# Eps inside the first part's statistics, logits scaled ahead of the shift, and the eighth gathered group on VectorE

## The reference, cut to what matters

```python
def layer_norm(x, g, b):
    mu = xf.mean(-1, keepdims=True)
    var = jnp.square(xf - mu).mean(-1, keepdims=True)
    return ((xf - mu) * lax.rsqrt(var + LN_EPS) * g + b).astype(x.dtype)

def route(xf, router_w, router_b):
    s = jax.nn.sigmoid((xf @ router_w).astype(jnp.float32))
    sb = (s + router_b).reshape(T, N_GROUPS, EXP_PER_GROUP)
    g_sel = jnp.argmax(lax.top_k(sb, 2)[0].sum(-1), axis=-1)      # best group of 8 experts
    ...                                                           # then the best two experts in it
def reference(...):
    for l in range(DEPTH):                                        # DEPTH = 2
        mix = hybrid_mixer(x, ...)
        x = layer_norm(ALPHA * x + mix, ln1_g[l], ln1_b[l])
        ffn = moe_ffn(x, router_w, router_b, moe_w1[l], moe_w3[l], moe_w2[l])   # 64 experts, 1024 -> 256 -> 1024
        x = layer_norm(ALPHA * x + ffn, ln2_g[l], ln2_b[l])
    return x
```

## Time and profile before

| | |
|---|---|
| three runs | 1145.03, 1145.22, 1147.53 us; median 1145.22 |
| profiled execution | 1146.11 us, of which 1143.2 us are the span from the first instruction to the last |
| busy, share of the span | PE 91%, PEld 50%, DVE 35%, ACT 24%, POOL 2% |
| DMA | 440.82 MB, mean 386 GB/s |
| the chain that ended last | PE 81%, DMA 10%, DVE 6%, issue 2% |
| mean granted TensorE clock | 0.993 |

### The profile page before, as it was taken

One profiled execution on the slowest core, in us unless ns is written; L12 is line 12 of the kernel. 1 busy time (PEld: TensorE's weight loads), 2 busy tenths in 40 slices (PEclk: granted clock), 3 DMA queues, 4 the chain that ended last, 5 costly groups with the idle time before them and its releaser, 6 DMA issues.

```text
span 1143.2 us, 32566 instructions
## 1 busy us (share of the span) xinstructions
PE 1045.1 (91%) x14230; PEld 573.9 (50%) x14230; DVE 405.7 (35%) x1207; ACT 270.9 (24%) x714; POOL 18.7 (2%) x36
## 2 busy tenths in 40 slices
PE   9999998899899899888899999988998998999887
PEld 6665754444445444444456657444454444444443
DVE  4875442222223222212268656322222222222223
ACT  1245331111121211111132544221212211111111
POOL 0010000000000000000000100000000000000000
PEclk9999999999999999989999999999999999999999
DMA  9968799999999999999996687999999999999997
GB/s 306 331 253 294 271 378 424 428 428 429 428 429 428 427 431 428 429 428 430 389 316 230 256 296 295 414 425 428 428 428 429 428 428 428 429 427 428 430 428 265
DMA packets 72047, 440.82 MB, mean 386 GB/s; under 512 B 16192, under 2 KB 39872, under 8 KB 45376
## 3 DMA queue, kind: packets, MB, share of 16 engines
q1 hardware_dynamic: 71712, 439.52, 94.1%
q0 software_dynamic: 144, 0.58, 0.1%
q10 hardware_dynamic: 144, 0.07, 0.0%
HBM read 439.10 MB, written 1.05 MB: 385 GB/s over the span
## 4 chain that ended last, share of the span: by engine, by line
PE 81%; DMA 10%; DVE 6%; issue 2%; SPq 1%; another core or an unknown queue 1%; ACT 0%; POOL 0%; DVEq 0%
PE bank L1179 16%; PE bank L1191 9%; PE bank L1070 9%; PE bank L1100 8%; PE bank L703 8%; PE bank L1090 8%; DMA w_even<-in_moe_w 4%; DMA w_odd<-in_moe_w 4%; PE bank L829 4%; PE bank L1142 3%; DVE moe L1696 2%; DVE moe L1754 1%; PE bank L974 1%; PE bank L1185 1%; DMA w_even<-in_w_in 1%
## 5 line engine op out<-in xcount | busy, mean ns | idle before, releaser
L1827 ACT ACTIVATE moe<-bank 128x512 f32<-128x512 f32 (+2 forms) x164 | 84.0, 523 | 546.8 <-PE bank L1090 227.3
L1696 DVE COPY moe<-bank 128x512 f32<-128x512 f32 (+1 forms) x66 | 44.6, 675 | 315.5 <-PE bank L1090 209.9
L1191 PE MATMUL bank<-moe 128*128 128x512 f32 (+1 forms) x264 | 119.5, 593 | 25.4 <-DVE moe L1754 22.5
L1070 PE MATMUL bank<-moe,x 128*64 128x64 f32 x3840 | 122.8, 224 | 3.7 <-issue 3.7
L1070 PEld LDWEIGHTS bank<-moe,x 128*64 128x64 f32 x3840 | 118.4, 139 | 6.9 <-issue 6.9
L1179 PE MATMUL bank<-w_even,moe 64*32 64x512 f32 x896 | 100.7, 598 | 10.4 <-DVE moe L1713 9.3
L1179 PE MATMUL bank<-w_odd,moe 64*32 64x512 f32 x896 | 99.6, 590 | 10.7 <-DVE moe L1713 8.7
L1987 ACT ACTIVATE moe<-bank,small 128x64 f32<-128x64 f32 x240 | 74.2, 414 | 110.5 <-PE bank L1070 110.5
L1191 PEld LDWEIGHTS bank<-moe 128*128 128x128 f32 x264 | 47.3, 189 | 99.7 <-DVE moe L1754 47.9
L1754 DVE COPY moe<-bank 128x512 f32<-128x512 f32 x28 | 19.3, 691 | 196.2 <-PE bank L1179 196.2
L703 PE MATMUL bank<-w_even,w_odd 128*128 128x384 f32 x240 | 81.3, 489 | 0.0
(11 more groups left out here) (202 smaller groups left out, 978.4 us busy)
## 6 DMA issues: line engine op xcount, KB each, us to landing
w_odd<-in_moe_w SPq DMA_DIRECT2D x86, 2048.0 KB, 29.3
w_even<-in_moe_w SPq DMA_DIRECT2D x82, 2048.0 KB, 30.4
w_even<-in_moe_w SPq DMA_DIRECT2D x28, 1024.0 KB, 8.8
w_even<-in_w_in SPq DMA_DIRECT2D x24, 768.0 KB, 10.8
w_odd<-in_moe_w SPq DMA_DIRECT2D x16, 1024.0 KB, 8.2
w_odd<-in_w_out SPq DMA_DIRECT2D x2, 2048.0 KB, 16.1
w_odd<-in_w_out SPq DMA_DIRECT2D x4, 1024.0 KB, 9.0
w_odd<-in_moe_w SPq DMA_DIRECT2D x8, 512.0 KB, 11.1
```

The lines of the kernel that those rows point to most:

```text
L1070: last = mm(bank[2 + h][64 * z:64 * z + 64, 64 * c:64 * c + 64], xc_pair[:, t, h, c, :], chosen_pair[:, t, z], start=t == 0, stop=t == 1)
L1191: return mm(Y[t][h][:, lo - 512 * h:hi - 512 * h], scatter[:, t * P:(t + 1) * P], y_rows[:, lo:hi], start=False, stop=True, skip_group_che ...
L1696: return nc.vector.tensor_copy(partial[:, k, cols], source[:, cols])
L1827: return fn(dst, src, ACT.Copy)
```

## The change

1. **Eps.** A new `add_eps(t, eps)` adds eps x 1024 to the sum of squares in the first part's statistics, right after that part's `bn_stats`. `moments` no longer adds eps; `bn_aggr` itself signals GpSimd, which reads the variance from `mean_var`. This holds for the two normalisations of both layers.
2. **Scores.** The logits are scaled first, and the shift is computed behind that with a signal of its own, `n_shift_ok`, for which ScalarE waits before it normalises the tile.
3. **Gather.** Group 7 goes to bank 6, which is otherwise unused at that time. VectorE scales it after its four others; ScalarE is left with 2, 3 and 6. The first product of the batch waits for groups 4 and 5 by `first_late_sb`, for 6 by `xg_act`, for 7 by `xg_dve`.
4. **Dummies.** Three instead of five ahead of the wait for `picked`.

```diff
+        first_part = [of[:, lo * P:(lo + 1) * P] for of, lo in ((bank[2], 0), (bank[2], 1), (bank[3], 0), (bank[3], 1),
+                                                                (bank[1], 2), (bank[1], 3), (bank[0], 2), (bank[6], 0))]
...
-                powers(1, 4, 1)
-                powers(2, 5, 1)
+                powers(1, rstd[:, 4:5], mean_var[:, 0, 1:2])
+                powers(2, rstd[:, 5:6], mean_var[:, 1, 1:2])
...
-                keep_warm(5, bank[7])
+                keep_warm(3, bank[7])
...
                         elif c == 4:
-                            pe.wait_ge(xg_dve.sem, b0 + 1)
+                            after(pe, l, first_late_sb, 1)
                         elif c == 6:
                             pe.wait_ge(xg_act.sem, b0 + 1)
+                        elif c == 7:
+                            pe.wait_ge(xg_dve.sem, b0 + 1)
...
-                def moments(t, o, eps, parts=2):
-                    link(nc.vector.bn_aggr(mean_var[:, t, :], stats[:, t, 0:parts, :].rearrange("p i s -> p (i s)")))
-                    ts(ms[:, o:o + 1], mean_var[:, t, 1:2], eps, None, ALU.add).then_inc(pow_in.sem, 1)
+                def add_eps(t, eps):
+                    link(ts(stats[:, t, 0, 2:3], stats[:, t, 0, 2:3], eps * DM, None, ALU.add))
+                def moments(t, n, parts=2):
+                    nc.vector.bn_aggr(mean_var[:, t, :], stats[:, t, 0:parts, :].rearrange("p i s -> p (i s)")
+                                      ).then_inc(pow_in.sem, 1)
+                    after(v, l, pow_in, n)
 
                 def scores(t):
                     after(v, l, pow_out, 2 + t)
-                    link(ts(shift[:, t:t + 1], mean_var[:, t, 0:1], rstd[:, 4 + t:5 + t], -1.0, ALU.mult, ALU.mult))
                     after(v, l, z_psum, t + 1)
                     after(v, l, logit_bias_ok, 1)
-                    signal(stt(out=ez[:, t, :], in0=bank[0][:, t * NE:(t + 1) * NE], scalar=rstd[:, 4 + t:5 + t],
-                               in1=logit_bias, op0=ALU.mult, op1=ALU.add), z_lin, t + 1)
+                    stt(out=ez[:, t, :], in0=bank[0][:, t * NE:(t + 1) * NE], scalar=rstd[:, 4 + t:5 + t],
+                        in1=logit_bias, op0=ALU.mult, op1=ALU.add).then_inc(z_lin.sem, 1)
+                    ts(shift[:, t:t + 1], mean_var[:, t, 0:1], rstd[:, 4 + t:5 + t], -1.0, ALU.mult, ALU.mult
+                       ).then_inc(n_shift_ok.sem, 1)
...
                 scale_first(4)
-                scale_first(5).then_inc(xg_dve.sem, 1)
+                scale_first(5).then_inc(first_late_sb.sem, 1)
+                v.wait_ge(gathered[1].sem, b0 + 1)
+                scale_first(7).then_inc(xg_dve.sem, 1)
...
                     fn(sg[:, t, :], ez[:, t, :], ACT.Sigmoid).then_inc(z_squashed.sem, 1)
+                    after(act, l, n_shift_ok, t + 1)
...
                 act.wait_ge(gathered[1].sem, b0 + 1)
-                scale_first(6)
-                scale_first(7).then_inc(xg_act.sem, 1)
+                scale_first(6).then_inc(xg_act.sem, 1)
```

More of the change, by code:

```diff
@@ L572, in _, with powers @@
             for l in range(DEPTH):
-                def powers(i, lo, n):
+                def powers(i, to, of):
                     after(pool, l, pow_in, i + 1)
-                    nc.gpsimd.tensor_tensor(rstd[:, lo:lo + n], ms[:, lo:lo + n], const("minus_half", 0, n),
-                                            ALU.pow).then_inc(pow_out.sem, 1)
-                powers(0, 0, 4)
+                    nc.gpsimd.tensor_tensor(to, of, const("minus_half", 0, of.shape[1]), ALU.pow).then_inc(pow_out.sem, 1)
+                powers(0, rstd[:, 0:4], ms[:, 0:4])
                 after(pool, l, router_in, 32)
@@ L609, in _ @@
                 total(pt(fold_mem[0], router[:, 0:4, :], router[:, 4:8, :], ALU.add), fold_mem[0][:, 0, :]).then_inc(sums_ok.sem, 1)
-                powers(1, 4, 1)
-                powers(2, 5, 1)
+                powers(1, rstd[:, 4:5], mean_var[:, 0, 1:2])
+                powers(2, rstd[:, 5:6], mean_var[:, 1, 1:2])
                 assert steps[0] == POOL_STEPS, steps
-                powers(3, 6, 1)
-                powers(4, 7, 1)
+                powers(3, rstd[:, 6:7], mean_var[:, 0, 1:2])
+                powers(4, rstd[:, 7:8], mean_var[:, 1, 1:2])
         @block.tensor
@@ L1038, in gather_first @@
                             after(pe, l, *((routed, 1) if t else (z_lin, 2)))
-                        last = mm(first_bank[c // 2][:, c % 2 * P:(c % 2 + 1) * P], xc[:, t, c, :], chosen[:, t, :],
-                                  start=t == 0 and c in (0, 2), stop=t == 1, skip_group_check=True)
+                        last = mm(first_part[c], xc[:, t, c, :], chosen[:, t, :],
+                                  start=t == 0 and c in (0, 2, DC - 1), stop=t == 1, skip_group_check=True)
                         if t == 1 and c % 2:
@@ L1651, in copy_gathered @@
                     last.then_inc(xg_dve.sem, 1)
-                for h in range(2):
-                    link(add_mix(0, h))
-                moments(0, 4, LN_EPS)
+                link(add_mix(0, 0))
+                add_eps(0, LN_EPS)
+                link(add_mix(0, 1))
+                moments(0, 2)
                 link(nc.vector.memset(find_one, BIG))
@@ L1663, in _ @@
                 link(add_mix(1, 0))
+                add_eps(1, LN_EPS)
                 signal(place(0), chosen_first, 1)
@@ L1666, in _ @@
                 link(add_quarter(3))
-                moments(1, 5, LN_EPS, 3)
+                moments(1, 3, 3)
                 weigh_scores(0)
@@ L1790, in _ @@
                     after(v, l, y_part, t + 1)
-                    part_sums(t, 0)
+                    link(part_sums(t, 0))
+                    add_eps(t, LN_EPS / ALPHA ** 2)
                 for t in range(NT):
```

11 lines of the change are left out of this document (6 added, 5 removed).

## The result

The changed kernel takes **1227.12 us** (median of five runs, 1223.00 to 1231.37) beside 1147.2 us for the kernel before on the same chip (five runs, 1145.03 to 1149.33): 1.0691 times the time, interval 1.0669 to 1.0713. The prediction said 1144.6 us with a range up to 1146.9. It forecast a gain of 0.6 us, and the change costs 80.

A forecast was written before the change was run, and what follows sets the result against it. Each layer was taken as a stretch bound by TensorE, then one bound by weight transfers. The terms summed to 2 x (0.06 + 0.14) + 0.19 = 0.59 us, from 1145.22 to 1144.6 us, range 1143.4 to 1146.9.

The forecast's parts named there:

- The step that failed: Ahead of the pick in the router: two dummies less hold back nothing and buy nothing, taken as 0.
- My slower rival: Router: TensorE's clock falls in the gap the dummies leave; up to 6.8 - 0.6 us lost, 1150 to 1151; chance 0.06.
- An instruction saved inside the batches is worth nothing: Batches of experts: DMA engines are full there, share 1.01, so saving an instruction gains nothing.
- What counts is when the stream starts: Router's end: issuing the weight load sooner than 148.16 moves the whole stream forward, until the last batch.
- `add_eps`: Both normalisations, both layers: eight small VectorE operations of 0.15 us, covered by waits; cost taken as nothing.
- Eps: Router, tile 1: without the eps addition in the chain GpSimd starts 0.18 us sooner.
- Scores: Router, tile 1: logits' scaling waits for the products, 0.12 us after their end; gain 0.06 us, bounds 0 and 0.43.
- Shift and gates: Router, behind the logits: the two VectorE instructions overlap and stay inside 0.40 us; taken as nothing, 0.10 us at worst.
- The eighth group: Gather: VectorE scales group 7, ready sooner than before; gain 0.14 us, bounds 0.05 and 0.25.
- The end of layer 0: Second normalisation, tile 0: GpSimd starts sooner, and normalising and transposes hang on it; gain 0.19 us.
- The end of layer 1: VectorE saves 0.17 to 0.19 us, but TensorE's last products wait for `ln_b`; gain 0, other bound 0.17.
- the first rival: Whole kernel: every removed instruction counts in full, 1.72 us gained, 1143.5 us; chance 0.10.

The follow-up runs named there:

- five-dummy kernel: Changed kernel with five dummies ahead of the pick instead of three: 1145.88 us, ratio 0.9988; with light w1 and w3 loads 1127.55 us, with w2 also cut 1126.70 us.
- 49 more: Kernel before with 49 instructions more at the start of TensorE's program: 1184.91 us, ratio 1.0342.
- 16 more in the body: Kernel before with 29 instructions more at the start, plus 16 more at the end of the loop's body: 1223.98 us, ratio 1.0686.

## Why the prediction was wrong, point by point

**The step that failed** is "two less (0.48 us) buy nothing but up to 0.1 us of a less filled array ... I take 0." As work on TensorE this was right: three dummies alone leave layer 0's loads 18.61 us apart as before, and in the changed kernel the rank's weights load 0.04 us behind the pick's end, after an idle stretch of 0.40 us:

```profile
143.35 0.20 DVE L1614 TENSOR_SCALAR moe<-moe 128x64 f32<-128x64 f32 x1
...
143.59 0.30 PEld L1053 LDWEIGHTS bank<-moe,constants 128*128 128x128 f32 x2 [0.40 <-DVE moe L1614]
```

What I did not cost is that a removed instruction also moves all code behind it. Sixteen places put layer 1's loop where each branch back fetches nine blocks again; the explanation that fits the places tried is that the body and the block behind it there need one block more than TensorE keeps. The two dummies alone give the loss (1231.17 us, where I had taken 0); so does moving the loop with the dummies in place; and 15 empty instructions take it away. No rival of mine had this mechanism. Nothing on the page of the kernel before warned of it; what could have been counted was a loop's body of 1704 instructions, 6.7 blocks.

The Trainium skill, "Runtime: NRT & Kernel Launch", section "Instruction fetch mechanics", has the matter: TensorE keeps 2048 instructions, refilled in blocks of 256, and a taken branch whose target is not in the current window stalls until it is fetched. The packets here (16.4 KB, nine a turn, a limit that fits eight blocks) agree. The same section puts that window at two pages. By this every branch back over 1704 instructions would stall, at any place; at 203, 211 and 254 none does, with 33 packets in all, so for TensorE the measurement decides for the larger figure. Such a stall took 8.5 to 9.3 us at the loop's head in the changed kernel.

**TensorE's clock.** My slower rival put the fall between 140 and 150 us, from the gap that the dummies leave. There the clock was not touched: the rank's two loads take 0.30 us as in the earlier trace rows. It did fall, as a consequence: after 9 us idle the clock over 800 to 806 us is 0.62 and the 64 products take 5.83 for 3.66 us, 14.5 us in the six turns. With the 4.7 us at L1183 it is about 19 of the 79 us, a quarter.

**"An instruction saved inside the batches is worth nothing"** was not tested: no run saves one there at a good place. What the runs show is how near TensorE is to the stream: in the five-dummy kernels, cutting most of the loads gave only 18 to 19 us. "What counts is when the stream starts" did not hold once TensorE stood still: in the changed kernel layer 1's first load is issued at 713.99 against 713.71 before, and the end is 79 us later. The forecast had that load 0.59 us sooner; it is 0.28 later.

**The small terms** can be read in the changed kernel's layer 0, relative to the combining of tile 1's parts:

```profile
138.71 1.29 PE L987 MATMUL bank<-moe,w_odd 128*128 128x64 f32 x8
138.77 0.24 DVE L1584 BATCH_NORM_AGGREGATE small<-small 128x2 f32<-128x18 f32 x1
...
139.09 0.59 POOL L578 TENSOR_TENSOR small<-small,constants 128x1 f32<-128x1 f32 x1 [15.97 <-DVE small L1584]
...
140.22 0.28 DVE L1592 SCALAR_TENSOR_TENSOR moe<-bank,small 128x64 f32<-128x64 f32 x1 [0.49 <-PE bank L987]
140.42 0.20 DVE L1594 TENSOR_SCALAR small<-small 128x1 f32<-128x1 f32 x1
...
140.54 0.25 DVE L1624 TENSOR_SCALAR moe<-moe,small 128x64 f32<-128x64 f32 x1
...
140.89 0.22 DVE L1599 TENSOR_TENSOR moe<-moe,small 128x64 f32<-128x64 f32 x1
```

- *`add_eps`.* Nothing, as taken: the combining starts 0.06 us after the router's last products do, as in the earlier trace rows.
- *Eps.* GpSimd starts 0.32 us after the start of the combining instead of 0.51: 0.19 sooner, 0.18 predicted.
- *Scores.* The scaling waits for the products, as said. But from their end (140.00) it takes 0.22 us, not the 0.12 of tile 0. So it starts 1.45 us after the combining instead of 1.41: a loss of 0.04 where I had a gain of 0.06.
- *Shift and gates* overlap: they start at 140.42 and 140.54, and the bias comes 0.67 us after the logits instead of 0.68. Nothing, as taken.
- *The eighth group.* From VectorE's `place` (L1635 at 144.07; before, L1625 at 143.94) to SP's load (148.07; 148.16) it is 4.00 us instead of 4.22: a gain of 0.22, where I had 0.14 within 0.05 to 0.25:

```profile
145.57 1.80 DVE L1696 TENSOR_SCALAR moe<-bank,small 128x128 f32<-128x128 f32 x5
145.87 1.35 ACT L2008 ACTIVATE moe<-bank,small 128x128 f32<-128x128 f32 x3
...
148.07 0.33 SPq L414 DMA_DIRECT2D w_even<-in_moe_w  x1
```

  From the combining to this load: 9.30 us instead of 9.49, in layer 0 and in layer 1 alike. 0.19 a layer, 0.20 predicted, but by luck: the loss at the scores and the larger gain at the eighth group cancel.
- *The end of layer 0.* From the combining to the first transpose 2.05 us instead of 2.24, the 0.19 predicted:

```profile
570.62 0.24 DVE L1584 BATCH_NORM_AGGREGATE small<-small 128x2 f32<-128x18 f32 x1
570.93 0.55 POOL L578 TENSOR_TENSOR small<-small,constants 128x1 f32<-128x1 f32 x1 [431.26 <-DVE small L1584]
...
572.67 0.44 PEld L656 LDWEIGHTS bank<-constants,x 128*128 128x128 f32 x3 [0.31 <-ACT x L1874]
```

- *The end of layer 1.* I took 0 within 0 to 0.17. From tile 0's combining to the first store of the output it is 4.02 us in the changed kernel (1213.12 to 1217.14) and 4.06 before (1134.47 to 1138.53): 0.04.

By rows the edits are thus worth 2 x 0.19 + 0.19 = 0.57 us. The five-dummy kernel agrees with it, though its interval cannot tell 0.6 us from 0.1 or 2.6. Whether 0.19 us at the load reach the end of the layer is not shown: in three kernels whose layer 0 is that of before, tile 0's parts are combined there at 569.47, 569.96 and 570.50 us, and the changed kernel's 570.62 and the five-dummy kernel's 569.12 lie on both sides of them. Layer 1's load fits: the changed kernel comes to that combining 0.66 us later than before, gains 0.19 there and 0.19 at the load, and issues it 0.28 us later.

Two sums of the prediction are slightly off, and nothing hangs on them: the first rival gives 1143.5, not the 1143.4 at the foot of the range, and the clock's full loss gives 1151.4 rather than 1150 to 1151.

**What stays open.** Why a body that begins 12 to 19 places too late (49 more) refetched in three turns and one that was 8 to 15 too late (16 more in the body) in all six; perhaps the branch comes, in some turns, before the block behind it is fetched, but no run tells. Why the head's wait differs so much between the places is open too. Also open is what fills the 3.1 us from one packet to the next, each of which takes 1 us, when the DMA engines are idle. The exact edges (between 195 and 203, and between 283 and 303) were not looked for, and no other length of body was tried than 1704 and 1720.

## What to carry to other kernels

Before costing an edit to an engine that runs a loop, count the instructions of the body and those ahead of it, in what the engine fetches: an edit of a few instructions anywhere ahead can move the loop over a block's edge and cost more than all the work it saves. Look at the packets of the instruction queue and at "issue" ahead of a loop's first instruction on the page; packets far above the program's length divided by 256 mean that the body is fetched anew. Where a body is near the limit, shorten it or keep its place with empty instructions, and compare variants only at places that are known to be good.

## What the runs showed of the hardware

- TensorE's loop of 1704 instructions ran undisturbed from the places 203, 210, 211, 240, 246, 254, 260, 261 and 283, and refetched nine blocks a turn from 195. At 303 it did so in three turns of six. With 1720 instructions, 256 was good and 283 bad.
- From place 195 a branch back cost 6.0 to 6.7 us with idle DMA engines and 8.5 to 10.3 with full ones (the changed kernel and the two kernels of before with the loop there), then 1.3 to 2.0 us later in the turn (L1169), and some 3 us from the lower clock, less a shorter wait for loads: 13 us in all, for nine packets that themselves take 1 us each. In layer 0, also with full DMA engines, the head's wait was 5.8 to 7.2 us (1720 instructions, place 283) and 4.3 to 4.7 (1704, place 303).
- While TensorE was stopped, the DMA share stayed at 1.01 for 9 us with weights issued earlier, and dropped to 0.79 over the next 6.
- After 9 us without work TensorE's granted clock was 0.62 over 6 us, a mix of its two levels; after the idle 0.40 us ahead of the rank its loads took what they took before.
